# Prompt attention by pairs of heads, with the last recurrence passes on GpSimd and the first cached keys turned early

## What is computed

```python
# prompt attention, 16 query heads on 4 key/value heads of 64
s = einsum('tcgd,scd->tcgs', q, k) * 64 ** -0.5          # causal; 512 positions are two blocks of 256
p = softmax(where(causal, s, -1e30)); o = einsum('tcgs,scd->tcgd', p, v)
# recurrence of the sample requests, a 64x64 state S per head and request, 4 steps
sa = einsum('bhij,bhj->bhi', S, -kk_t)
S = S * w_t[:, :, None, :] + sa[..., :, None] * (kk_t * a_t)[..., None, :] + v_t[..., :, None] * k_t[..., None, :]
o_t = einsum('bhij,bhj->bhi', S, r_t)
# sample attention: per request the 3 best of 16 cached blocks by the query's product with the block's mean key
```

## Time and profile before

| | |
|---|---|
| median of 3 runs | 3066.37 us (3065.93 to 3068.41) |
| the profiled execution | 3062.45 us, span 3060.8 us |
| TensorE busy | 2962.2 us, 97% of the span |
| VectorE, ScalarE, GpSimd busy | 2008.7 us (66%), 833.2 us (27%), 298.1 us (10%) |
| the chain that ended last | TensorE 82%, VectorE 11%, ScalarE 2% |
| DMA | 322.59 MB, mean 105 GB/s |

### The profile page before, as it was taken

The page is one execution under the profiler, slowest core; times in us unless marked ns, Lnnn a source line. Parts: engine busy times, 40 slices in busy tenths (PEclk is TensorE's granted clock), DMA queues, the critical chain, the costliest instruction groups (busy, mean ns, idle before and its releaser), DMA issues.

```text
span 3060.8 us, 53510 instructions
## 1 busy us (share of the span) xinstructions
PE 2962.2 (97%) x20734; PEld 2408.1 (79%) x20734; DVE 2008.7 (66%) x3792; ACT 833.2 (27%) x1945; POOL 298.1 (10%) x520
## 2 busy tenths in 40 slices
PE   8999999999999899998999999999999999999997
PEld 7888778778775677786888888888888877888776
DVE  4444566657998433257767667676676689787888
ACT  1000144431327544203222222222222233222234
POOL 0000011110001455232000000000000000000002
PEclk9999999999999999998999999999999999999999
DMA  6333000013212799821233232332323235343221
GB/s 190 83 83 82 19 10 11 9 36 93 70 43 67 230 282 286 258 65 63 78 124 110 88 128 84 118 116 82 128 86 115 94 117 184 98 139 100 88 88 73
DMA packets 338063, 322.59 MB, mean 105 GB/s; under 512 B 20601, under 2 KB 323686, under 8 KB 336408
## 3 DMA queue, kind: packets, MB, share of 16 engines
q1 hardware_dynamic: 323284, 278.66, 29.4%
q0 software_dynamic: 14528, 40.52, 4.2%
HBM read 296.37 MB, written 22.74 MB: 104 GB/s over the span
## 4 chain that ended last, share of the span: by engine, by line
PE 82%; DVE 11%; issue 3%; ACT 2%; DMA 1%; POOL 0%; POOLq 0%; SPq 0%; DVEq 0%; ACTq 0%
PE ps L1357 46%; PE ps L845 11%; PE ps L914 7%; PE ps L1327 4%; PE ps L1172 4%; PE ps L773 2%; PE ps L1213 1%; PE ps L1268 1%; PE ps L1120 1%; PE ps L1225 1%; PE ps L1158 1%; DVE BIG L2392 1%; PE ps L1251 0%; ACT BIG L1817 0%; ACT BIG L1799 0%
## 5 line engine op out<-in xcount | busy, mean ns | idle before, releaser
L1357 PE MATMUL ps<-BIG,UA 128*128 128x272 f32 x2288 | 538.9, 392 | 0.4 <-ACT UV L1970 0.4
L1357 PEld LDWEIGHTS ps<-BIG,UA 128*128 128x128 f32 x2288 | 434.6, 190 | 90.4 <-issue 0.8
L1357 PE MATMUL ps<-XT,UA 128*128 128x272 f32 x1400 | 331.6, 392 | 0.0
L1357 PEld LDWEIGHTS ps<-XT,UA 128*128 128x128 f32 x1400 | 266.0, 190 | 54.8
L1357 PE MATMUL ps<-BIG,DA 128*128 128x272 f32 x1200 | 293.7, 393 | 9.6 <-ACT UV L2071 3.4
L1357 PEld LDWEIGHTS ps<-BIG,DA 128*128 128x128 f32 x1200 | 226.5, 190 | 59.9 <-issue 12.2
L773 PE MATMUL ps<-XT,W 128*128 128x272 f32 x768 | 181.6, 397 | 0.7 <-ACT W L1749 0.7
L773 PEld LDWEIGHTS ps<-XT,W 128*128 128x128 f32 x768 | 147.5, 193 | 35.5 <-issue 4.8
L914 PE MATMUL ps<-BIG 64*64 64x64 f32 (+1 forms) x3072 | 148.4, 236 | 21.5 <-DVE BIG L2392 12.7
L914 PEld LDWEIGHTS ps<-BIG 64*64 64x64 f32 x3072 | 130.3, 139 | 35.6 <-DVE BIG L2392 19.7
L3507 POOL COPY CVT<-GP 128x2 f32<-128x2 f32 x44 | 15.5, 352 | 1005.6 <-DVE GP L2958 822.3
(11 more groups left out here) (657 smaller groups left out, 5418.4 us busy)
## 6 DMA issues: line engine op xcount, KB each, us to landing
BIG<-in_w_up_dram SPq DMA_DIRECT2D x176, 512.0 KB, 5.5
W<-in_w_in_dram SPq DMA_DIRECT2D x38, 1024.0 KB, 5.8
BIG<-in_w_down_dram SPq DMA_DIRECT2D x96, 384.0 KB, 3.9
W<-in_cache_k_dram SPq DMA_DIRECT2D x128, 128.0 KB, 3.5
W<-in_cache_k_dram POOLq DMA_DIRECT2D x128, 128.0 KB, 3.6
W<-in_cache_v_dram SPq DMA_DIRECT2D x128, 128.0 KB, 3.4
W<-in_cache_v_dram POOLq DMA_DIRECT2D x128, 128.0 KB, 3.5
h_keep<-H SPq DMA_DIRECT2D x22, 544.0 KB, 2.7
```

Source lines behind the costliest of these rows:

```text
L1357: last = nc.tensor.matmul(ps[:, bank, 0:HALF], weights[:, k], x[:, k], start=start and k == 0, stop=k == kc - 1, skip_group_check=not start)
```

## The change

- **TensorE, order of the scores.** `pair_scores(q, group)` takes the place of `head_scores(n)`: the scores of heads 2q and 2q + 1 in turn, in three groups (both blocks 3; both blocks 2; the four small ones, which share the banks 2, 3 and 6). Each has a bank of its own or waits: the second 256-column score waits for the first, which is in the same bank. Group 1 of the next pair is issued between the turned parts of head a, group 2 between those of head b, group 0 of the pair after that behind the values' product.
- **TensorE, turned weights.** `turn_head(n, part)` writes to the banks 4 and 5 in turn (before: 4, 5 and 6) and waits for the copy two parts before.
- **ScalarE** follows with the copies (`turned_head`), the output and the exponentials in the new order; the exponentials of a pair stand behind one another.
- **VectorE** makes two divisions and then two masked maxima, and waits for whole banks (`BANK_WHOLE`). `HEAD_PASSES` is `{6: 2}`: of the recurrence one pass (a tensor_reduce) is left, behind head 6. The sample's queries are laid out behind heads 7, 9 and 11 (before: 12, 13 and 14).
- **GpSimd** makes the four passes before that one (subtract, multiply, add, multiply, each over 128 x 2048), one behind the other, behind the last rotation (`rope_ev`).
- **The cached keys.** `turn_keys(0)` is issued ahead of the last pair, behind the last masked maximum.

```diff
         BLOCKS = (3, 2, 1, 0)
+        SCORES = (((0, 3, 0, 0), (1, 3, 1, 0)), ((0, 2, 2, 0), (1, 2, 3, 0)), ((0, 1, 6, 0), (1, 0, 3, 384), (0, 0, 2, 384), (1, 1, 6, 256)))
+        SCORE_AT = {(e, i): (bank, at) for group in SCORES for e, i, bank, at in group}
+        SCORE_BANKS = [bank for group in SCORES for e, i, bank, at in group]
+        BANK_WHOLE = {bank: k + 1 for k, bank in enumerate(SCORE_BANKS)}
...
+        rec_pool, REC_POOL = S["pair_pool"], PAIRS + 1
...
+            def pair_scores(q, group):
+                for e, i, bank, at in SCORES[group]:
+                    rows = slice(e * 64, e * 64 + 64)
+                    if q:
+                        pe.wait_ge(S["max_ev"], 8 * q - 7 + 4 * e if group == 0 else 8 * q)
+                    if (e, i) == (1, 1):
+                        pe.wait_ge(S["sc_mm"], 8 * q + 5)
+                    nc.tensor.matmul(ps[:, bank, at:at + (i + 1) * P], ZT[rows, q, i * P:(i + 1) * P], KDUP[rows, q // 2, 0:(i + 1) * P],
                                      start=True, stop=True).then_inc(S["sc_mm"], 1)
...
+            def turn_head(n, part):
+                m = 3 * n + part
+                if m > 1:
+                    pe.wait_ge(S["pt_ev"], m - 1)
+                for a in ((0,), (1,), (2, 3))[part]:
                     for i in range(a, 4):
                         off = i * (i + 1) // 2 * P
                         o = (2 if a == 3 else i - a) * P
...
+                        last = nc.tensor.transpose(ps[:, 4 + m % 2, o:o + P], PR[n % 3][:, off + a * P:off + (a + 1) * P], ident)
+                last.then_inc(S["pt_mm"], 1)
+            pe.wait_ge(acc_free, RW_TILES + ATT_TILES + 1)
+            pe.wait_ge(acc_free, RW_TILES + ATT_TILES + 2)
+            pair_scores(0, 0)
+            pair_scores(0, 1)
+            rotate(len(ROPE_TILES) - 1)
+            pe.wait_ge(S["kvt_ev"], 5)
+            pair_scores(0, 2)
+            pair_scores(1, 0)
+            def turn_keys(t):
...
+            for q in range(8):
+                a, b, v = 2 * q, 2 * q + 1, q // 2
+                if q == 7:
+                    pe.wait_ge(S["max_ev"], 64)
+                    turn_keys(0)
+                if q == 0:
+                    pe.wait_ge(S["rope_ev"], 10)
+                    pe.wait_ge(S["gn_root"], 2 * PAIRS)
+                    nc.tensor.matmul(ps[:, 7, 0:256], const("swap"), ZT[:, 0:8, SEQ:TOK], start=True, stop=True).then_inc(S["swap_mm"], 1)
+                pe.wait_ge(S["pnorm_ev"], a + 1)
+                turn_head(a, 0)
+                turn_head(a, 1)
+                if q < 7:
+                    pair_scores(q + 1, 1)
+                turn_head(a, 2)
+                pe.wait_ge(S["pnorm_ev"], b + 1)
+                turn_head(b, 0)
+                if q < 7:
+                    pair_scores(q + 1, 2)
+                turn_head(b, 1)
+                turn_head(b, 2)
+                if q:
+                    pe.wait_ge(S["ao_ev"], q)
+                else:
                     pe.wait_ge(S["qsw_ev"], 1)
...
+                for x in range(4):
+                    pe.wait_ge(S["pt_ev"], 3 * b + min(x, 2) + 1)
+                    toff = sum(4 - y for y in range(x)) * P
                     for h in range(2):
...
+                        last = nc.tensor.matmul(ps[64 * h:64 * h + 64, 7, x * P:512], KVT[:, x, 256 + v * HD:256 + (v + 1) * HD],
+                                                PT[h][:, toff:toff + (4 - x) * P], start=x == 0, stop=x == 3, skip_group_check=True)
                 last.then_inc(S["ao_mm"], 1)
...
+                if q < 6:
+                    pair_scores(q + 2, 0)
...
             for t in range(CACHE_SLOTS):
                 v = t - V_FROM
-                if t < 32:
+                if 0 < t < 32:
                     turn_keys(t)
...
+            def turned_head(n, part):
+                m = 3 * n + part
+                act.wait_ge(S["pt_mm"], m + 1)
+                toff, w = ((0, 4 * P), (4 * P, 3 * P), (7 * P, 3 * P))[part]
+                nc.scalar.activation(PT[n % 2][:, toff:toff + w], ps[:, 4 + m % 2, 0:w], ACT.Copy).then_inc(S["pt_ev"], 1)
+            for q in range(8):
+                a, b = 2 * q, 2 * q + 1
+                turned_head(a, 0)
+                turned_head(a, 1)
+                if q:
+                    output(q - 1)
+                turned_head(a, 2)
+                turned_head(b, 0)
+                if q < 7:
+                    block_exps(b + 1, 0)
+                turned_head(b, 1)
+                if q < 7:
+                    block_exps(b + 1, 1)
+                turned_head(b, 2)
+                if q < 7:
+                    block_exps(b + 1, 2)
+                    block_exps(b + 1, 3)
+                    for k in range(4):
+                        block_exps(b + 2, k)
...
-                        yield link(nc.vector.tensor_tensor(SDh, SDh, TD, ALU.subtract))
-                        yield link(nc.vector.tensor_tensor(TD, rows_of(v[:, half * 32:half * 32 + 32]), cols(k, 32), ALU.mult))
-                        yield link(nc.vector.tensor_tensor(SDh, SDh, TD, ALU.add))
-                        yield link(nc.vector.tensor_tensor(TD, SDh, cols(r, 32), ALU.mult))
+                        if half == 1 and t == DEC_SEQ - 1:
+                            last_step[0] = linked[0]
+                            dve.wait_ge(rec_pool, REC_POOL + 4)
+                        else:
+                            yield link(nc.vector.tensor_tensor(SDh, SDh, TD, ALU.subtract))
+                            yield link(nc.vector.tensor_tensor(TD, rows_of(v[:, half * 32:half * 32 + 32]), cols(k, 32), ALU.mult))
+                            yield link(nc.vector.tensor_tensor(SDh, SDh, TD, ALU.add))
+                            yield link(nc.vector.tensor_tensor(TD, SDh, cols(r, 32), ALU.mult))
                         yield link(nc.vector.tensor_reduce(OD[:, t, half * 32:half * 32 + 32], TD, AX, ALU.add))
...
+                    bank, at = SCORE_AT[n % 2, i]
+                    dve.wait_ge(S["sc_mm"], 8 * (n // 2) + BANK_WHOLE[bank])
                     off = i * (i + 1) // 2 * P
...
+                    nc.vector.tensor_tensor_reduce(out=PR[n % 3][:, off:off + (i + 1) * P], in0=ps[:, bank, at:at + (i + 1) * P],
...
-            HEAD_PASSES = {1: 1, 3: 1, 5: 1, 7: 1, 9: 2}
+            HEAD_PASSES = {6: 2}
             LAST_PASS = max(HEAD_PASSES)
...
-                if n < 14:
+                if n % 2 and n < 15:
+                    masked_max(n + 1)
                     masked_max(n + 2)
                 recur(HEAD_PASSES.get(n, 0))
-                if n == 12:
+                if n == 7:
...
-                if n in (13, 14):
+                if n in (9, 11):
...
-                    sample_queries(n - 13)
+                    sample_queries((n - 9) // 2)
...
+            r, k, v = (SV[:, j, DEC_SEQ - 1] for j in range(3))
+            cols = lambda x: x.rearrange("p (a j) -> p a j", a=1).to_broadcast([P, 32, HD])
+            v_rows = v[:, 32:64].rearrange("p (i a) -> p i a", a=1).to_broadcast([P, 32, HD])
+            pool.wait_ge(S["dve_chain"], last_step[0])
+            pool.wait_ge(S["rope_ev"], len(ROPE_TILES))
+            nc.gpsimd.tensor_tensor(SD[1], SD[1], TD, ALU.subtract).then_inc(rec_pool, 1)
+            pool.wait_ge(rec_pool, REC_POOL + 1)
+            nc.gpsimd.tensor_tensor(TD, v_rows, cols(k), ALU.mult).then_inc(rec_pool, 1)
+            pool.wait_ge(rec_pool, REC_POOL + 2)
+            nc.gpsimd.tensor_tensor(SD[1], SD[1], TD, ALU.add).then_inc(rec_pool, 1)
+            pool.wait_ge(rec_pool, REC_POOL + 3)
+            nc.gpsimd.tensor_tensor(TD, SD[1], cols(r), ALU.mult).then_inc(rec_pool, 1)
```

## The result

The changed kernel takes 3071.28 us (median of 15 runs, 3065.76 to 3075.74) beside 3065.85 us of the kernel before (median of 15 runs in turn with them, 3061.66 to 3071.2): a ratio of 1.0021, 95% interval 1.0013 to 1.0028, so 6.4 us slower (4.0 to 8.6). Measured once more on another occasion it was 1.0029 (1.0017 to 1.0042). The forecast was 13.6 us slower: the direction holds, but the size is less than half of it. The profiled execution took 3075.74 us with a span of 3074.1.

The account below looks back on a forecast made before the run. TensorE, busy nearly all the time, and prompt attention's chain of waits were the bound. The second key turns moved from 1007.37 to 1021.4, 14.0 later, with 0.4 coming back: 3066.4 + 13.6 = 3080 us, range 3061 to 3088.

Parts of the forecast that it names:

- head 0 turns: Start of attention: TensorE turns head 0's first block at 947.0, after a VectorE stall of 18.5 us from 928.5.
- to head 2's turn: First pair: 8.7 us less an output of 0.5, plus 3 for a slow clock, from 947.0 to 958.2.
- to the second key turns: Remaining attention: six periods to 1010.4, reduce and small copies to 1013.4, last pair 8.0 to 1021.4.
- part 1: TensorE, scores of two heads in turn: they overlap, a pair's scores taking 2.5 us, bounds 2.5 and 4.7.
- part 2: New order within a pair: period 8.7 us against 10.23, or 9.3 if scores don't overlap; floor 7.3.
- part 3: Start: VectorE stands some 2 us in masked maximum 0; TensorE could turn head 0 at 928.5, about as now.
- part 4: GpSimd's four passes, 5.06 us each, alternate with VectorE's division tensor_scalar: stall 18.5 us, bounds 0 and 21.7.
- Rival (b): VectorE keeps the path for all four tensor_scalar; each pass delays one division, 11 us in all, 3072.5; chance 0.13.
- The slow clock: First pair after TensorE's 18 us pause: 3 us added for the lower clock, bounds 0 and 7.
- The reduce: VectorE's remaining 2.29 us pass between the divisions of heads 6 and 7, where 0.6 is free: costs 1.7 us.
- Rival (a): GpSimd's passes don't hold the divisions up: 3080 - 18.5 = 3061.5 us, not slower; chance 0.16.
- the case that had 0.68: Start of attention: the stall comes in full, including scores that don't overlap; 3074 to 3088 us, chance 0.68.

Follow-up runs that it names:

- without the passes: Changed kernel with GpSimd's four recurrence passes replaced by their signal, the reduce staying on VectorE; ratio 0.9970 to the kernel before.
- the gated kernel: Changed kernel with GpSimd's four passes waiting for 2, 4, 6 and 8 divisions and the reduce moved behind head 8; ratio 0.9967 to the kernel before.
- the reduce in a wait: Changed kernel with VectorE's reduce moved from behind head 6 to behind head 8's first masked maximum; ratio 1.0015 to the kernel before.
- the kernel in quarters: Changed kernel with each of GpSimd's four passes issued as four instructions of 512 columns; ratio 1.0001 to the kernel before.
- the keys turned late: Changed kernel with the first cached keys' turn put back behind the last output; ratio 1.0034 to the kernel before.
- the division by tensor_tensor: Changed kernel with the scaling in divisions 0 and 1 written as tensor_tensor with broadcast reciprocal instead of tensor_scalar; ratio 1.0036 to the kernel before.
- all passes on VectorE: Changed kernel with the four passes back on VectorE, in its waits at heads 0, 2, 4, 6, and the reduce at head 8; ratio 0.9967, measured twice.

## Why the prediction was off

The stretch by the prediction's own steps, all counted from the rotation's sum (918.19 before, 915.62 after):

| step | predicted | changed | without the passes |
|---|---|---|---|
| head 0 turns | 947.0 - 918.19 = 28.8 | 21.0 | 11.4 |
| to head 2's turn | 958.2 - 947.0 = 11.2 | 13.3 | 10.1 |
| to the second key turns | 1021.4 - 958.2 = 63.2 | 65.2 | 62.5 |
| sum | 103.2 | 99.5 | 84.0 |

**The scores (part 1): right.** Two scores of 512 columns, one of either head, take 1.1 us in the changed kernel (four instructions at 948.85, 1.13 us) where one head's takes 0.94. They overlap.

**The period (part 2): right.** 8.7 predicted; 8.61 and 8.70 measured ahead of the pair with the reduce, 9.00 and 8.92 behind it; 8.70 in the gated kernel from the second pair to the reduce.

**The start (part 3): nearly right.** VectorE waits 2.73 us inside masked maximum 0, some 2 predicted. Without the passes head 0 turns 11.4 behind the sum, 10.3 predicted: 1.1 late. There TensorE is busy at a clock of 0.50 just ahead of that turn, not waiting for the division.

**The stall (part 4): the mechanism right, the size wrong.** This is the step that failed, a term of the sum that was mis-sized: 18.5 us predicted, some 11.5 measured. 9.6 of them lie before head 0's turn, by the kernel without the passes. The pair behind that turn takes 13.3 us against 10.1 there, 3.2 more, but not all of it is hold-up: with the reduce in a wait, where the passes hold head 1 up just as long and the clock is full from 944 us on, it takes 12.0. So 1.9 us are head 1's division and 1.3 the clock. There are two reasons for the smaller size, in the term's two factors. A pass takes 4.49 to 4.57 us, and the product of two broadcast inputs 3.74, not 5.06: four times the 512-wide instruction counts its fixed part four times, as the kernel in quarters shows, where three of its passes took 4.96 to 5.13 us. The Trainium skill (GPSIMD Engine Reference, Elementwise — side-by-side cycle accounting) gives 4497 ns, and the trace agrees. The second reason is the strict turns: two tensor_scalar went ahead in the first gap, so four passes met only three of division 0, and the fourth pass met division 1 at its first instruction, where 1.9 of its 4.1 us were on the path. Rival (b) named 11 us, the size that came, but by another course: all four tensor_scalar in a row, each pass delaying one division. The lengths 3.77 and 4.72 of single instructions within a division decide against it, so its number is luck. Why the second went through in the first gap and none did so later, no run tells.

**The slow clock: right in the first pair, missing behind the reduce.** 3 us were counted in the first pair, over 8.2 at full speed. Without the passes that pair takes 10.1, 1.9 over, with the clock at 0.50 until about 930; in the changed kernel the clock takes 1.3 more, so 3.2. In its three other profiles the pair took 13.2, 14.8 and 15.9 us, so the term is 3 to 6 us from one execution to the next, within the bounds of 0 and 7. It cost 2.8 us behind the reduce besides, where none was counted.

**The reduce: right alone, wrong in the changed kernel.** 1.7 us was predicted. Without the passes the pair takes 10.5 against 8.7, 1.8 us. In all four profiles of the changed kernel it takes 13.3 to 13.5, with the clock at 0.72 in the stretch around it, and 13.3 to 13.4 in the kernels with the passes in quarters, gated, with the keys turned late and with the division by tensor_tensor. The gated kernel has no stall ahead of it, so the stall isn't what makes it long. Moved into a wait for scores, the clock stayed at 1.00. What makes the clock fall after the same wait of 1.71 us in these kernels and not in the one without the passes is open.

**The baseline: the second error.** In the sum the stall was 7.0 us too large, the start 1.1 and the reduce with its clock 2.9 too small, and the remaining steps differ by some 0.7. These steps take the forecast for the stretch from 14.0 us longer to 10.3. The rest lies in the kernel before: 89.2 us was its favourable case, 93.3 its case in two of three profiles. Against that the changed kernel's 99.4 to 102.1 are 6 to 9 us longer, and the measured difference is 6.4 and 8.9. The prediction had read the slow clock in 924 to 926 as part of the kernel before, and didn't ask how long it lasts in other executions: its length differs by 10 us between the profiles of that kernel. Bounds for the clock belonged on both kernels.

**Rival (a)** gave the time without the hold-up as 4.9 us below the kernel before. Measured it is 9.2 to 10.1 below, in the kernel without the passes, the gated one and the one with all passes on VectorE; 4.1 of the difference is the same baseline. Its stretch, 103.2 - 18.5 = 84.7 us, is within 0.7 of the 84.0 measured without the passes.

**The chances.** "Slower" had 0.73 and came true, near its lower bound of 0.2%. 3071.3 us lies within the range of 3061 to 3088, but below the 3074 to 3088 of the case that had 0.68 and was forecast; it lies where rival (b), with 0.13, put it. The direction was less safe than 0.73 says: with a stall of 11.5 us and the baseline corrected, 13.6 becomes 2.5 us, less than a measurement can tell, and only the 1.1 and 2.9 us that the prediction missed at the start and at the reduce bring it to some 6. One reading of the trace was a slip: the prediction says that the trace has the case with at most 544 columns, and the tensor_scalar of the earlier trace rows has 560.

## What to carry to other kernels

Work given to GpSimd isn't off VectorE's path if both read SBUF by the path they share: in these traces the passes were covered only where VectorE ran no tensor_scalar of the fast form and nothing with two SBUF inputs meanwhile. Put each such pass behind the point where VectorE turns to PSUM work (here worth some 16 us, 1.0021 against 0.9967, with a one-line wait each), or keep it on VectorE in a wait that is there anyway. And before a few microseconds are forecast from one profile, ask which stretches of it run at the lower clock, and treat their length as a spread on both sides of the comparison.

## What was not expected of the hardware

- An instruction that waits for the shared path is shown as running: a tensor_scalar of 512 columns took 4.72 us, 0.483 alone; VectorE's busy share rose to 98% in a stretch in which TensorE starved.
- The exclusion isn't bound to the fast form: tensor_tensor with both inputs in SBUF took 12.07 us for four beside the same passes, while masked maxima reading PSUM and one SBUF operand kept their 0.69 us and a reciprocal of 4 columns its 0.16 to 0.18.
- Exclusion in turns isn't strict: in the gap behind the first pass two tensor_scalar got through, in each later gap one; the pattern repeated to 0.01 us in four profiles.
- GpSimd's tensor_tensor of 2048 columns took 4.49 to 4.57 us in the changed kernel with two full inputs or one broadcast one, and 3.62 (gated) and 3.74 with two broadcast ones; in quarters 4.96 to 5.13 and 4.27.
- The kernel before ran at the lower clock for 10 us in one execution and 20 in two others at the start of attention, behind a pause of TensorE at the rotation that is the same in both (10.2 us busy of 12 in 908 to 920), with TensorE busy all the while, and that is worth 4.1 us.
